# A diffusion block on one Trainium2 core: Hyena spectra from even and odd times, and scan outputs turned within the next group's steps

## The chip, the cores and the metric

The kernel runs on one core of one Trainium2 chip, all in fp32. The metric is the device time of an execution in microseconds. PE is TensorE, DVE is VectorE, ACT is ScalarE, POOL is GpSimd and SP is the engine that issues most of the transfers. The kernel is written instruction by instruction: each engine has its own program, and the programs meet only at semaphores.

## What is computed

One layer of a backbone with 256 latent and 256 context tokens of width 2048. Two parts of it matter here, the Hyena convolution and the output of the gated delta scan:

```python
def hyena_filters(n, w1, b1, w2, b2, w3, b3, freq):
    ...
    filt = filt * jnp.exp(-t[:, None] * deltas[None, :])[:, None, None, :]
    circ = jnp.concatenate([filt[:, 0], jnp.zeros((1, HY_ORDER, HY_W), F32), filt[:0:-1, 1]], axis=0)
    return jnp.fft.rfft(circ, axis=0)

def long_conv(u, filt_f, skip):
    n = u.shape[1]
    y = jnp.fft.irfft(jnp.fft.rfft(u, n=2 * n, axis=1) * filt_f, n=2 * n, axis=1)[:, :n]
    return y + u * skip.astype(F32)

def hyena_mix(p, conv, conv_w, filt_f, skip):
    ...
    y = x1 * long_conv(v, filt_f[:, 0], skip[0])
    return x2 * long_conv(y, filt_f[:, 1], skip[1])

def gated_delta_chunked(q, k, v, g, beta, s0):      # per head and direction, chunks of 64 tokens
    ...
    def step(s, inp):
        q_i, k_i, u_i, w_i, g_i, a_i = inp
        v_new = u_i - jnp.einsum('bhcd,bhdv->bhcv', w_i, s)
        o = jnp.einsum('bhcd,bhdv->bhcv', q_i * jnp.exp(g_i)[..., None], s) + jnp.einsum('bhcm,bhmv->bhcv', a_i, v_new)
        ...
        return s, o

def merge_branches(o_dn, proj, y_hy, norm_w, w_pa, w_ph, w_out):
    z = ...
    o = (rms_norm(o_dn.transpose(0, 2, 1, 3), norm_w) * jax.nn.silu(z)).reshape(b, n, DN_V_W).astype(dt)
    gates = jax.nn.sigmoid(proj[..., OFF_GATE:].astype(F32))
    merged = gates[..., :D_MODEL] * (o @ w_pa) + gates[..., D_MODEL:] * (y_hy.astype(dt) @ w_ph)
    return merged.astype(dt) @ w_out
```

After that come an output projection, a layer norm and the PEER feed-forward, which gathers rows of two expert tables and fills the second third of the time.

## The kernel before

The stages follow each other: modulation, gates, projection and short convolution of 16 heads (to 883 us), gates (to 1092), the 48 Hyena tiles of the combined projection (to 1430), the Hyena convolutions (to 1661), the scan (to 1871), the 32 tiles of the branch projections (to 2096), output projection and norm, and PEER (from 2242). Each Hyena tile of the first 32 is turned to tokens on partitions by two PE transposes (`hy_turn`, L678, from `hacc`).

**Hyena convolutions.** The 2048 channels go in four blocks `n` of 512, and each has two orders `o`, so `convolve(n, o, last)` runs eight times, six of them in a loop. A transform is a product with a constant matrix of cosines or sines: 256 times on the contraction (two halves `t` of 128), 256 frequencies (two halves `f`), 512 channels on the free side. On PE the order in `convolve` is: the filter's spectrum, four banks of two accumulated products each (L710; banks 4, 5 the cosines of the sum filter `fa`, banks 6, 7 the sines of `fb`); the signal's transform, eight products into banks 0 to 3 (L720); `filters` for the next convolution (L700, into banks 4 to 7); the inverse (L733 for o = 0, L740 for o = 1). ACT copies the four banks of the spectrum to `Fr` and `Fi` (L1012, L1013). DVE runs `products` (L1400 to L1408, six operations for each half `f`), then `fold`, which makes the next `fa` and `fb` out of `filters` (L1378 to L1389), then the multiplication by the gate (L1415, or L1420 into `yhT`). PE waits for `fold` before the spectrum (`fil_used`), for the last gate product before the signal (`inv_used`), for the copies before `filters` (`spec_copied`), and for all products before the inverse (`prod_done`).

**Scan.** 16 heads go in four groups of four (`grp`), in a loop of two passes with two groups each (`r`). A group has eight steps `g`: four over the context, four over the latent tokens. In a step PE multiplies keys (and queries) by the states (L771, L774), DVE makes `r_in` (L1446), PE multiplies it by the inverses (L784), ACT copies and scales the result (L1025, L1028), PE multiplies by the attention (L792, latent only) and by the keys (L804), and DVE updates the states (L1466) and adds the outputs to `o_acc` (L1474). The first step of a group has no state and begins with L784. A group ends with: the squares of `o_acc` (L1032) and the root (L1035) on ACT, the reciprocal (L1476) and the scaling (L1481) on DVE, PE's transposes of `o_acc` (L809) and DVE's products with `zsT` (L1488), which count `o_merged`. The first L784 of the next group waits for `o_merged`; so do SP's loads of the inverses of the group after (`inverses_in`, 32 transfers into one of two `invs`), POOL's loads of `att` (one buffer, 16 transfers) and of the records two groups ahead (`rec_load`).

**Branches.** `wide(s, s, ...)` makes one tile of 16 products into bank `s`; its weights come from four slots of `wring`, which share their place with scan records, so SP loads them only after PE has counted `br_proj` at the scan's end. Tiles alternate between delta output (`zsT`) and Hyena output (`yhT`), and DVE multiplies by the gates and adds.

Of the kernel before, what the change touches and what calls it, by code (L numbers as in the profile page):

```python
# [22 lines left out]
ALU = mybir.AluOpType  # L23
# [3 lines left out]
P = 128  # L27
D = 2048
KT = D // P
# [17 lines left out]

CONST_COLS = {}
# [10 lines left out]
def constant_table():  # L59
# [24 lines left out]
    two = lambda a: a.reshape(2, P, SEQ).transpose(1, 0, 2).reshape(P, 2 * SEQ)  # L84
    put("cos", two(np.cos(ang)))
# [9 lines left out]
def build(nc, a, out):  # L95

    with ExitStack() as ctx:
# [136 lines left out]
        yb = area(HT0 + 12288, 2, N1)  # L234
        zT = area(R0 + 17024, SEQ)
# [15 lines left out]
        invs = [area(at, 4, 1024).rearrange("p u (q t w i) -> p u q t w i", q=2, t=2, w=2) for at in (HT0, R0 + 20480)]  # L251
        att = area(R0 + 28672, 4, 512).rearrange("p u (t w i) -> p u t w i", t=2, w=2)
# [8 lines left out]
        tmp_g = area(R0 + 28672, 2, SEQ)  # L261
# [87 lines left out]
        def _(sp):  # L349
# [139 lines left out]
        def _(pe):  # L489
# [213 lines left out]
            def convolve(n, o, last):  # L703
# [19 lines left out]
                if not last:  # L723

                    pe.wait_ge(sem("spec_copied"), c * 4 + 4)
# [26 lines left out]
            with pe.Fori(0, 2) as i:  # L752
                for r in range(2):
# [5 lines left out]
                    for g in range(8):  # L759
# [4 lines left out]
                        for u in range(4):  # L764
# [41 lines left out]
                    for u in range(4):  # L806
                        pe.wait_ge(sem("o_normed"), grp * 8 + (2 * u + 2))
                        for t in range(2):
                            m = nc.tensor.transpose(bank[2 * u + 1][:, (2 + t) * P:(3 + t) * P], o_acc[:, 2 * u + t, :], const("ident"))  # L809
                        m.then_inc(sem("o_turned"), 1)  # L810
# [1059 lines left out]
```

## Time and profile before

| | us |
|---|---|
| three runs | 3635.89, 3638.99, 3639.49 |
| median | 3638.99 |
| profiled execution, its own time | 3637.51 |
| its span | 3636.0 |
| PE busy | 2911.1 (80%) |
| DVE busy | 2172.2 (60%) |
| ACT busy | 393.8 (11%) |
| POOL busy | 977.5 (27%) |
| mean granted clock of PE | 0.882 |

"Idle before" is the time that an engine stood still ahead of an instruction, with the instruction on another engine that ended it; "issue" is waiting that nothing in the trace accounts for.

### The profile page before, as it was taken

To read this page: it belongs to the slowest core of one execution; us is meant where nothing else is said; L and a number is where in the kernel's file an instruction comes from. 1 tells how busy PE (TensorE), PEld (TensorE's weight loads), DVE (VectorE), ACT (ScalarE), POOL (GpSimd) and SP (SyncE) were. 2 spreads that over 40 slices of the span, in tenths; PEclk is the share of its full clock that TensorE was granted. 3 is DMA by queue.
4 is the path that set the end of the run, shared out by engine and by line. 5 is a ranking of instruction groups with operands and counts; after the bars stand their busy time and mean duration, and the time that the engine had idled before them with its cause. 6 is when DMAs were issued, how large, how long until landed. Compare 5 with 4: busy or idle time off the path is not lost.

```text
span 3636.0 us, 33108 instructions
## 1 busy us (share of the span) xinstructions
PE 2911.1 (80%) x10631; PEld 1816.6 (50%) x10631; DVE 2172.2 (60%) x3251; ACT 393.8 (11%) x951; POOL 977.5 (27%) x752
## 2 busy tenths in 40 slices
PE   4899999999999999998789997665565655556555
PEld 1585555556888887445678845542222222222222
DVE  1236767676997122655640013796878778886675
ACT  0121222222000000002310000010000000000000
POOL 0000111111000001001100000377666566666552
PEclk7899999999999999999899998877768677777777
DMA  9335666667444442103324543899999999999997
GB/s 410 150 118 209 225 229 225 241 223 265 172 173 174 150 155 93 35 23 108 103 99 151 207 162 118 342 407 417 422 422 421 421 421 422 385 421 422 421 422 304
DMA packets 146743, 935.09 MB, mean 257 GB/s; under 512 B 35295, under 2 KB 35584, under 8 KB 38356
## 3 DMA queue, kind: packets, MB, share of 16 engines
q0 software_dynamic: 92384, 652.43, 44.2%
q1 hardware_dynamic: 54264, 281.52, 21.1%
q8 instruction: 45, 0.74, 0.1%
q14 instruction: 50, 0.41, 0.0%
HBM read 906.51 MB, written 27.36 MB: 257 GB/s over the span
## 4 chain that ended last, share of the span: by engine, by line
PE 57%; DMA 21%; DVE 10%; issue 6%; POOL 5%; DVEq 0%; ACT 0%; SPq 0%; PEld 0%; POOLq 0%; ACTq 0%; PEldq 0%
PE bank L534 25%; PE bank L595 15%; DMA arena<-peer_v_in,arena 15%; POOL arena L1801 5%; PE bank L865 4%; DMA arena<-peer_u_in,arena 3%; PE bank L831 3%; DMA arena<-w_ada_in 3%; DVE arena L1637 2%; PE bank L710 2%; PE bank L784 1%; DVE arena L1658 1%; PE bank L740 1%; PE bank L733 1%; PE bank L720 1%
## 5 line engine op out<-in xcount | busy, mean ns | idle before, releaser
L865 PE MATMUL bank<-arena 128*128 128x512 f32 x992 | 700.9, 873 | 517.7 <-DMA arena<-peer_v_in,arena 488.2
L534 PE MATMUL bank<-arena 128*128 128x256 f32 x4608 | 1008.4, 381 | 9.2 <-DMA arena<-w_branch_in 5.1
L534 PEld LDWEIGHTS bank<-arena 128*128 128x128 f32 x4608 | 876.2, 191 | 131.2 <-issue 8.7
L865 PEld LDWEIGHTS bank<-arena 128*128 128x128 f32 x992 | 270.4, 286 | 947.5 <-issue 902.7
L1637 DVE CUSTOM_DVE_ANT_0 arena<-arena 128x2048 f32<-128x2048 f32 x256 | 587.0, 2293 | 246.4 <-DMA arena<-peer_u_in,arena 223.5
L1801 POOL DMA_INDIRECT arena<-peer_u_in,arena x256 | 387.0, 1512 | 776.4 <-issue 548.5
L595 PE MATMUL bank<-arena 128*128 128x512 f32 (+1 forms) x1536 | 556.3, 522 | 0.0
L1801 POOL DMA_INDIRECT arena<-peer_v_in,arena x256 | 440.4, 1720 | 163.4 <-issue 74.0
L595 PEld LDWEIGHTS bank<-arena 128*128 128x128 f32 x1536 | 290.7, 190 | 258.8 <-issue 241.8
L1658 DVE SCALAR_TENSOR_TENSOR arena<-arena 128x2048 f32<-128x2048 f32 x130 | 305.7, 2352 | 41.4 <-DMA arena<-peer_v_in,arena 37.3
L1260 DVE CUSTOM_DVE_ANT_0 arena<-arena 128x2048 f32<-128x2048 f32 x64 | 146.6, 2290 | 138.8 <-DMA arena<-w_ada_in 138.8
L1715 POOL DMA_DIRECT2D arena<-w_ada_in x64 | 34.3, 535 | 615.9 <-DVE arena L1260 422.0
L1362 DVE TENSOR_SCALAR arena<-arena 128x256 f32<-128x256 f32 (+1 forms) x48 | 16.9, 352 | 205.2 <-PE bank L678 135.2
L831 PE MATMUL bank<-arena 128*128 128x512 f32 x256 | 112.4, 600 | 9.5 <-DVE arena L1519 8.1
L1334 DVE TENSOR_TENSOR arena<-arena 128x62 f32<-128x62 f32 (+30 forms) x124 | 106.6, 859 | 17.1 <-DMA arena<-beta_scr 12.9
L1337 DVE TENSOR_TENSOR arena<-arena 128x62 f32<-128x62 f32 (+30 forms) x124 | 106.6, 860 | 4.3
L1246 DVE SCALAR_TENSOR_TENSOR arena<-arena 128x256 f32<-128x256 f32 x192 | 91.9, 479 | 9.1 <-DVE arena L1244 2.3
L505 PE MATMUL bank<-arena 128*32 128x512 f32 x256 | 47.4, 878 | 48.2 <-DMA arena<-w_ada_in 48.2
L831 PEld LDWEIGHTS bank<-arena 128*128 128x128 f32 x256 | 48.9, 192 | 72.6 <-issue 61.9
L1068 ACT ACTIVATE arena<-arena 128x16 f32<-128x16 f32 x16 | 3.5, 216 | 704.4 <-DVE arena L1637 704.4
L1272 DVE RECIPROCAL arena<-arena 128x256 f32<-128x256 f32 (+1 forms) x32 | 79.3, 2521 | 0.2 <-DVE arena L1266 0.2
L1766 POOL MEMSET arena<- 128x2048 f32 x1 | 1.8, 1804 | 281.3 <-DVE arena L1364 281.3
(253 smaller groups left out, 2235.8 us busy)
## 6 DMA issues: line engine op xcount, KB each, us to landing
arena<-w_in_in SPq DMA_DIRECT2D x144, 1024.0 KB, 4.8
arena<-w_ada_in POOLq DMA_DIRECT2D x64, 1024.0 KB, 5.1
arena<-w_ada_in SPq DMA_DIRECT2D x16, 2048.0 KB, 17.2
arena<-w_branch_in SPq DMA_DIRECT2D x32, 1024.0 KB, 4.8
rec_scr<-arena POOLq DMA_DIRECT2D x16, 1024.0 KB, 4.6
arena<-rec_scr POOLq DMA_DIRECT2D x16, 1024.0 KB, 7.4
arena<-w_out_in SPq DMA_DIRECT2D x8, 2048.0 KB, 8.2
arena<-w_q_in SPq DMA_DIRECT2D x16, 1024.0 KB, 8.1
```

Of the source, the lines that this page charges most:

```text
L534: m = mm(bank[b][:, 0:SEQ], wring[:, slot, k, :], src[:, k, 0:SEQ], start=(k == 0), stop=(k == KT - 1))
L595: m = mm(bank[t][:, 0:n], wring[:, t, k, :], hT[:, k, 0:n], start=(k == 0), stop=(k == KT - 1))
L831: m = mm(bank[4 + t][:, :], gT[:, s * 8 + k, t * P:(t + 1) * P], wo_ring[:, s, k, :], start=(s == 0 and k == 0), stop=(s == 1 and k == 7))
L865: m = mm(bank[4 * t + j][:, :], diag[:, d % 8, :], ring[buffer[n]][:, j * N1:(j + 1) * N1], start=(d == 0 or d == last_pe[0] + 1), stop=(d ...
L1246: stt(a_lat, x, w(j), a_lat, ALU.mult, ALU.add).then_inc(sem("tap"), 1)
L1260: v.tensor_tensor_reduce(ada_junk, wring[:, 3].rearrange("p k n -> p (k n)"), cond_row, 1.0, 0.0, ALU.mult, ALU.add, ada_dot[:, e:e + 1]). ...
L1272: v.reciprocal(nrm[:, j, 0:n], nrm[:, j, 0:n]).then_inc(sem("recip"), 1)
L1334: tt(tmp, m_[:, j + 1:CH, j:j + 1].broadcast_to([P, rows, j]), m_[:, j:j + 1, 0:j].broadcast_to([P, rows, j]), ALU.mult).then_inc(sem("sol ...
L1337: tt(below, below, tmp, ALU.add).then_inc(sem("solve_step"), 1)
L1637: v.tensor_tensor_reduce(junk, ring[buffer[n]], h2[:, g // PH, :], 1.0, 0.0, ALU.mult, ALU.add, dots[:, g % 2, e:e + 1]).then_inc(sem("row ...
L1658: stt(y, ring[buffer[n]], c_, y, ALU.mult, ALU.add).then_inc(sem("row_dve"), 1)
L1801: pool.indirect_dma_start(ring[buffer[n]], None, a["peer_" + kind], bass.IndirectOffsetOnAxis(ap=idx[:, g // PH, at:at + 1].bitcast(U32), ...
```

## The change

Two things, and some that follow from them.

1. Tokens are put in the order even, then odd, on the contraction, and the upper half of the frequencies is mirrored (`EVEN_ODD`, `MIRRORED`). With that the two halves of a real transform are the sum and the difference of the even tokens' product and the odd tokens' product. The spectrum takes four products in place of eight (each bank holds one, nothing is accumulated), ACT copies the two odd banks only, and DVE makes `Fr` and `Fi` by four additions and subtractions (`spectra`). The signal's transform and the inverse keep their counts; `hy_turn` reads every second token, and the last gate product (L1420) reads its bank with a step of 128.
2. The end of group `grp` is moved into group `grp + 1`: squares on ACT after the copies of steps 0 and 1, the root after step 1, reciprocal and scaling on DVE at the end of step 1, transposes on PE in step 3 after each head's state products, and the products with `zsT` on DVE in step 3 before each head's `r_in`. The first L784 of a group waits for the additions of the one before only. The loop over groups is written out, so heads are constants. SP's and POOL's loads wait for `av_ready`, the last attention product of the group.
3. The branch tiles of each four are now two of Hyena, then two of delta output, so that the first two can run while the last group's outputs are finished; its transposes stand between tiles 0 and 1. DVE's operations on them are in the new order, without `tmp_g`.

```diff
+EVEN_ODD = np.arange(SEQ).reshape(P, 2).T.reshape(-1)
+MIRRORED = np.concatenate([np.arange(P), np.arange(SEQ - 1, P - 1, -1)])
...
+    ang = ang[EVEN_ODD][:, MIRRORED]
...
+        def out_at(grp, u, t):
+
+            return bank[4 + u][:, t * P:(t + 1) * P] if grp == 3 else bank[2 * u + t][:, (3 - t) * P:(4 - t) * P]
...
-                sp.wait_ge(sem("o_merged"), 5 + 4 * (grp - 1))
+                sp.wait_ge(sem("av_ready"), 16 * (grp - 1))
...
-                    m = nc.tensor.transpose(bank[4 + s][:, t * P:(t + 1) * P], hacc[:, s, t * P:(t + 1) * P], const("ident"))
+                    m = nc.tensor.transpose(bank[4 + s][:, t * P:(t + 1) * P], hacc[:, s, t::2], const("ident"))
...
-                for f in range(2):
-                    for src, w, b in ((fa, "cos", 4), (fb, "sin", 6)):
-                        for t in range(2):
-                            m = mm(bank[b + f][:, :], const(w)[:, t * SEQ + f * P:t * SEQ + (f + 1) * P], src[:, t, :],
-                                   start=(t == 0), stop=(t == 1))
+                for src, w, b in ((fa, "cos", 4), (fb, "sin", 6)):
+                    for t in range(2):
+                        m = mm(bank[b + t][:, :], const(w)[:, t * SEQ:t * SEQ + P], src[:, t, :], start=True, stop=True)
                     m.then_inc(sem("spec_ready"), 1)
...
+            def turn_out(grp, u):
+                pe.wait_ge(sem("o_normed"), grp * 8 + (2 * u + 2))
+                for t in range(2):
+                    m = nc.tensor.transpose(out_at(grp, u, t), o_acc[:, 2 * u + t, :], const("ident"))
+                m.then_inc(sem("o_turned"), 1)
...
+                            if g == 3 and grp:
+                                turn_out(grp - 1, u)
...
-                                pe.wait_ge(sem("o_merged"), 5 + grp * 4)
+                                if grp:
+                                    pe.wait_ge(sem("o_added"), grp * 32)
...
             pe.sem_inc(sem("br_proj"), 4)
+
+            def branches(i, s):
+                weights_in(s, i + 24)
+                pe.wait_ge(sem("br_used"), 1 + i * 4 + s)
+                wide(s, s, yhT if s < 2 else zsT).then_inc(sem("br_proj"), 1)
+
+            pe.wait_ge(sem("o_added"), 4 * 32)
+            branches(0, 0)
+            for u in range(4):
+                turn_out(3, u)
+            branches(0, 1)
             pe.wait_ge(sem("o_merged"), 5 + 16)
...
+                    for i in range(2):
+                        act.wait_ge(sem("spec_ready"), n * 4 + (2 * o + i + 1))
+                        act.wait_ge(sem("spec_copied"), n * 8 + (1 + 4 * o))
+                        af(odds[:, i, :], bank[5 + 2 * i][:, :], ACT.Copy).then_inc(sem("odd_copied"), 1)
...
+                    if grp and g < 2:
+                        squares(grp - 1, 2 * g)
+                        squares(grp - 1, 2 * g + 1)
+                        if g == 1:
+                            deviations(grp - 1)
...
+            def spectra(n, o):
+
+                c = n * 2 + o
+                for i, (F, b) in enumerate(((Fr, 4), (Fi, 6))):
+                    dve.wait_ge(sem("odd_copied"), c * 2 + (i + 1))
+                    even = bank[b][:, :]
+                    tt(F[:, 0, :], even, odds[:, i, :], ALU.add).then_inc(sem("spec_copied"), 1)
+                    if i == 0:
+                        tt(F[:, 1, :], even, odds[:, i, :], ALU.subtract).then_inc(sem("spec_copied"), 1)
+                    else:
+                        tt(F[:, 1, :], odds[:, i, :], even, ALU.subtract).then_inc(sem("spec_copied"), 1)
...
-                        tt(x, bank[b][:, 0:SEQ].unsqueeze(1), x, ALU.mult).then_inc(sem("inv_used"), 1)
+                        x = x.rearrange("p o (n t) -> p (o n) t", t=2)
+                        tt(x, bank[b][:, 0:SEQ].rearrange("p (t n) -> p n t", t=2), x, ALU.mult).then_inc(sem("inv_used"), 1)
...
+                            if g == 3 and grp:
+                                merge_out(grp - 1, u)
                             dve.wait_ge(sem("ks_ready"), grp * 28 + ((g - 1) * 4 + u + 1))
...
+                        if g == 1 and grp:
+                            normalize_out(grp - 1)
+            normalize_out(3)
+            for u in range(4):
+                merge_out(3, u)
```

`squares`, `deviations`, `normalize_out` and `merge_out` hold the operations that stood at a group's end, unchanged.

## Rows read from the trace of the kernel before

**Rows 1.** The page's chain that ended last: shares of the span by line.
```profile
PE bank L534 25%; PE bank L595 15%; DMA arena<-peer_v_in,arena 15%; POOL arena L1801 5%; PE bank L865 4%; DMA arena<-peer_u_in,arena 3%; PE bank L831 3%; DMA arena<-w_ada_in 3%; DVE arena L1637 2%; PE bank L710 2%; PE bank L784 1%; DVE arena L1658 1%; PE bank L740 1%; PE bank L733 1%; PE bank L720 1%
```
**Rows 2.** Windows: stretch, length; PE, PEld, DVE, ACT, POOL busy; granted clock, DMA, GB/s.
```profile
1440.37:1660.24 219.87, 205.13 (x504) 103.69 (x504) 113.35 (x182) 17.36 (x32) 9.42 (x17) 0.93 0.14 40
1661.11:1703.61 42.50, 38.63 (x384) 29.02 (x384) 29.34 (x116) 13.53 (x48) 5.46 (x5) 1.00 0.38 125
1712.07:1754.79 42.72, 39.92 (x384) 30.69 (x384) 29.59 (x116) 12.57 (x47) 11.61 (x20) 0.95 0.45 137
1763.96:1808.11 44.15, 40.89 (x384) 31.37 (x384) 29.80 (x116) 13.53 (x48) 9.88 (x18) 0.92 0.44 131
1816.58:1859.83 43.25, 40.50 (x384) 31.31 (x384) 29.77 (x116) 12.58 (x47) 9.47 (x16) 0.94 0.05 14
1859.83:1870.87 11.04, 1.97 (x9) 1.38 (x9) 3.93 (x17) 2.91 (x15) 0.00 (x0) 0.64 0.39 143
1542.00:1548.00 6.00, 5.37 (x13) 4.29 (x14) 5.71 (x10) 0.00 (x0) 0.00 (x0) 0.50 0.00 0
```
**Rows 3.** Chain in order of time, 1496 to 1556 us: start, length, what.
```profile
1498.25 6.87 PE bank L710 x16
1505.12 3.45 PE bank L720 x8
...
1516.87 7.13 PE bank L733 x16
1524.01 6.87 PE bank L710 x16
...
1542.63 10.22 PE bank L740 x32
```
**Rows 4.** Timeline, 1496 to 1556 us: start, length, instructions, idle before them in brackets.
```profile
1501.81 0.60 ACT L1012 ACTIVATE arena<-bank 128x512 f32<-128x512 f32 x1 [24.42 <-PE bank L710]
...
1508.78 0.69 DVE L1400 TENSOR_TENSOR arena<-bank,arena 128x512 f32<-128x512 f32 x1 [9.94 <-PE bank L720]
...
1516.87 7.13 PE L733 MATMUL bank<-arena 128*128 128x512 f32 x16 [1.46 <-DVE arena L1408]
```
**Rows 5.** Timeline, the end of the first group.
```profile
1702.97 0.31 ACT L1032 ACTIVATE arena<-arena 128x128 f32<-128x128 f32 x1 [0.36 <-DVE arena L1474]
...
1706.43 1.28 ACT L1035 ACT_TABLE_LOAD   x1
...
1708.29 1.66 DVE L1481 TENSOR_SCALAR arena<-arena 128x128 f32<-128x128 f32 x8
...
1709.87 2.15 DVE L1488 SCALAR_TENSOR_TENSOR arena<-bank,arena 128x128 f32 x8
```
**Rows 6.** Timeline, steps 1 and 2 of the second group.
```profile
1717.74 1.14 ACT L1025 ACTIVATE arena<-bank,arena 128x128 f32<-128x128 f32 x4 [3.09 <-PE bank L784]
...
1718.94 2.22 DVE L1466 SCALAR_TENSOR_TENSOR arena<-arena,bank 128x128 f32<-128x128 f32 x8 [1.12 <-PE bank L804]
...
1723.33 2.15 DVE L1466 SCALAR_TENSOR_TENSOR arena<-arena,bank 128x128 f32<-128x128 f32 x8 [1.12 <-PE bank L804]
```
**Rows 7.** Chain in order of time, from the second group to the third.
```profile
1761.94 2.02 issue
...
1766.07 0.05 ACTq L1025
```
**Rows 8.** Turned and straight operands on DVE (lines' own view), then the projection's chain.
```profile
L1344 DVE TENSOR_TENSOR arena<-arena x2: 7233/7240/7246, 1016.2 to 1139.0; 64x4096 f32<-64x4096 f32 x2
L1345 DVE TENSOR_TENSOR arena<-arena x2: 4422/4422/4422, 1023.5 to 1146.3; 64x4096 f32<-64x4096 f32 x2
1161.36 6.91 PE bank L534 x32
1168.49 6.91 PE bank L534 x32
```
**Rows 9.** Timeline, the end of the scan: SP's loads of branch weights.
```profile
1865.41 22.81 SPq L452 DMA_DIRECT2D arena<-w_branch_in  x6
```

More of the change, by code:

```diff
@@ L805, in _ @@
                                 m.then_inc(sem("upd_ready"), 1)
[L806 to L810, printed above, removed]
-            pe.sem_inc(sem("br_proj"), 4)
+            pe.sem_inc(sem("br_proj"), 4)
+            def branches(i, s):
[7 more added lines that the diff above has]
+            branches(0, 1)
             pe.wait_ge(sem("o_merged"), 5 + 16)
-            with pe.Fori(0, 8) as i:
+            branches(0, 2)
+            branches(0, 3)
+            with pe.Fori(1, 8) as i:
                 for s in range(4):
-                    weights_in(s, i + 24)
-                    pe.wait_ge(sem("br_used"), 1 + i * 4 + s)
-                    wide(s, s, (zsT, yhT)[s % 2]).then_inc(sem("br_proj"), 1)
+                    branches(i, s)
             pe.sem_inc(sem("wo_used"), 2)
@@ new lines, in _, with squares @@
+                    for i in range(2):
+                        act.wait_ge(sem("spec_ready"), n * 4 + (2 * o + i + 1))
+                        act.wait_ge(sem("spec_copied"), n * 8 + (1 + 4 * o))
+                        af(odds[:, i, :], bank[5 + 2 * i][:, :], ACT.Copy).then_inc(sem("odd_copied"), 1)
+            def squares(grp, u):
+                act.wait_ge(sem("o_added"), grp * 32 + (24 + 4 + u + 1))
+                for t in range(2):
+                    af(o_sq, o_acc[:, 2 * u + t, :], ACT.Square, accum_out=o_ss[:, 2 * u + t:2 * u + t + 1]
+                       ).then_inc(sem("o_ss"), 1)
+                    act.wait_ge(sem("o_ss"), grp * 9 + (2 * u + t + 1))
@@ L1036, in _ @@
+            for u in range(4):
+                squares(3, u)
+            deviations(3)
             for t in range(2):
@@ L1428, in _, with normalize_out, merge_out @@
             dve.wait_ge(sem("hpads"), 2)
-            with dve.Fori(0, 2) as i:
+            def normalize_out(grp):
+                dve.wait_ge(sem("o_ss"), grp * 9 + 9)
+                v.reciprocal(o_ss, o_ss).then_inc(sem("o_rstd"), 1)
+                dve.wait_ge(sem("o_rstd"), grp + 1)
+                for u in range(4):
+                    for t in range(2):
+                        oa = o_acc[:, 2 * u + t, :]
+                        ts(oa, oa, o_ss[:, 2 * u + t:2 * u + t + 1], None, ALU.mult).then_inc(sem("o_normed"), 1)
+            def merge_out(grp, u):
+                dve.wait_ge(sem("o_turned"), 1 + grp * 4 + (u + 1))
+                z_ = zsT[:, 4 * grp + u, :].rearrange("p (c n) -> p c n", c=NCH)
+                for t, zz in ((0, z_[:, 0::3, :]), (1, z_[:, 1:3, :])):
+                    m = stt(zz, out_at(grp, u, t).rearrange("p (c n) -> p c n", c=2), dn_nw[:, 0:1], zz,
+                            ALU.mult, ALU.mult)
+                m.then_inc(sem("o_merged"), 1)
+            for i in range(2):
                 for r in range(2):
@@ L1474, in _ @@
                                 tt(oa, bank[2 * u + 1][:, P:2 * P], oa, ALU.add).then_inc(sem("o_added"), 1)
-                    dve.wait_ge(sem("o_ss"), grp * 9 + 9)
-                    v.reciprocal(o_ss, o_ss).then_inc(sem("o_rstd"), 1)
-                    dve.wait_ge(sem("o_rstd"), grp + 1)
-                    for u in range(4):
-                        for t in range(2):
-                            oa = o_acc[:, 2 * u + t, :]
-                            ts(oa, oa, o_ss[:, 2 * u + t:2 * u + t + 1], None, ALU.mult).then_inc(sem("o_normed"), 1)
```

90 lines of the change are left out of this document (35 added, 55 removed).

## The prediction

> **What bounds the kernel now.** I read the page's chain of work that ended last first [rows 1]: PE's matmul lines lead it and DMA of the expert tables follows, so the time is a row of stages, each with its own limit, and a stage that gets shorter moves all later ones. Two stages are touched, and the windows give them [rows 2]: the Hyena convolutions, 219.87 us for eight of them, and the scan, four groups of heads with bodies of 42.50, 42.72, 44.15 and 43.25 us, gaps between them of 8.46 (1703.61 to 1712.07), 9.17 and 8.47, and 11.04 from the last body to the first branch matmul. In the windows of the bodies PE is busy over 90% of the time, but that counts pipelined latencies; so inside a stage I go by the chain of waits in order of time.
>
> In a convolution the chain is [rows 3]: spectra of the filter on PE (L710, 6.87 us for eight 128x512 products, two records each), the first half of the signal's transform (L720, 3.45), some 8.3 us of products on DVE while PE finishes the other half and the next filter (1508.56 to 1516.87), and the inverse on PE (L733, 7.13, or L740, 10.22). One convolution is 25.76 us (1498.25 to 1524.01); its partner is longer by what L740 is longer than L733. DVE sat idle 9.94 us before its products and the copies of ACT take 0.60 each [rows 4]: all of the spectra is on PE's side of the chain.
>
> In the scan each of a body's first four steps is a ring PE, DVE, PE, ACT, PE, DVE, 4.39 us long (the updates of the states begin at 1718.94 and 1723.33), with no engine the bound [rows 6]; the last four are longer rings of the same kind. Between groups the ring is empty: ACT squares o_acc, takes a root, DVE scales (L1481), PE turns, DVE merges (L1488), and only then does PE begin the next group [rows 5].
>
> **Spectra.** Removed: 4 of 8 products on PE per convolution. 6.87 / 8 = 0.86 each, so 3.43 us, at the head of the chain, with nothing else at work beside them. Added: ACT copies two odd banks in place of four, DVE makes four sums. Where do they lie? Let a convolution start at 0. The cosine pair is ready at 1.7, the sine pair at 3.4; ACT adds 0.6 to each; a 512-wide DVE operation comes every 0.6 to 0.7 (the run of products above has 12 in 8.3). The sums end near 5.5. The first half of the signal's transform now ends at 3.43 + 3.45 = 6.9. So 1.4 us of slack hides the sums in DVE's former idle time, of which 9.94 becomes about 6.5 less 2.7. If that cover were gone the four sums would cost up to 2.7 us each convolution, and the gain would fall to under 1. DVE's load for a convolution goes from 14.2 us (113.35 / 8 [rows 2]) to some 17 of 22.3, so it doesn't become the bound; PE waits for the products as before. Late next is what was late before: the products. The other order of frequencies, the even-odd windows and the once longer wait of PE's filters on the sums (queued behind it: only the inverse, which waits for the products anyhow) change no length. 8 x 3.43 = 27.4 us.
>
> **Strides.** The reads of odd or even tokens are the unknown costs. DVE: L1420's operand is now read with its inner step 128 elements long. The nearest rows are the same multiply of 64x4096 with turned operands, 7.24 us, and with straight ones, 4.42 [rows 8]: 2.82 / 4096 = 0.69 ns an element, so 0.18 us for 256, between 0 and 0.18; three of four hide under the next of PE's products, and the fourth is on the path only at the end: 0.2 us at most, which I take. PE: 64 transposes of the projection (L678) now read every second element. That stage is PE's alone: a tile comes every 7.13 us, of which 6.91 are its product and 0.22 a pair of transposes [rows 8]. No row has a PE operand with such a step; bounds are 0 and doubling, 32 x 0.22 = 7.0 us; a gain has no way to arise, since as many elements pass. I take 0, since the plain transposes are the nearest row, and keep 7.0 for the range. The Trainium skill speaks for 0 ("SBUF — State Buffer", Door 1, the note on cachelines): an SBUF line has 16 bytes and two hits in it are enough for the full rate, which a step of two fp32 gives. By it the sum stays; no row here shows it.
>
> **Scan, removed.** The three gaps go: 8.46 + 9.17 + 8.47 = 26.1, of which 0.1 each stays, since PE's first product of a group now waits only for the sums of the one before. The 9.17 has the loop's way back in it, which the unrolled code lacks; so I set all of it at nothing. Group one has no slow start but waits about 1.2 for a table load in ACT (1.28 [rows 5]): a clean body is 41.3. The others ran at a granted clock of 0.95, 0.92 and 0.94, because PE had stood still in the gap [rows 2], and lost 1.4 to 2.9 each. Unrolled, the registers that picked the head go too: in the step they stood on the chain before ACT's first operation, 0.05 us [rows 7], and in the same way before DVE's, with an issue of that size beside each. That is an estimate of 0.2 a step (bounds 0.1 and 0.3), for 7 steps of 4 groups: 5.6 us.
>
> **Scan, added.** The step is a ring, so whatever DVE does between two of its turns is paid whole. After step 1: reciprocal 0.2 and L1481, 1.66 [rows 5]: 1.9 us, ahead of L1446 of step 2, for which PE waits (its inverse products queue behind). Is the root ready? ACT has 3.09 idle before a step [rows 6]; eight squares took from 1702.97 to 1706.43, so four take 1.7, and fit beside step 0; four and the root, 2.0, fit beside step 1. But a table load in front of the root makes it 3.3 and DVE waits 1.15. Before, ACT loaded two tables in each pass of the loop over two groups (at its first copy, and at the root [rows 5]); straight code needs the second once: only the second group pays. In step 3: PE's two transposes for each head (0.22, as in the projection) fit between its products with the states, which come with the states, every 2.15 / 4 = 0.54 [rows 6]; DVE's two merges for each head come before that head's L1446: 2.15 us in all [rows 5], paid whole. So bodies: 42.5; 41.3 + 1.9 + 2.15 + 1.15 = 46.5; 45.35; 45.35. With 0.3 for three joints 180.0, against 198.72: 18.7 less, and the 5.6 of registers.
>
> PE now stands still twice in a group, 2 to 3 us, where before it stood 8 once. At the end of each product phase it idled 1.46 us [rows 4], and after every second one it was granted 0.50, the 1.2 GHz level [rows 2], so that L740 took 10.22 where L733, with as many columns, took 7.13 [rows 3]. So such stops can cost the clock. I allow two falls at the 2 us that the slow bodies lost: 4 us. Scan: 18.7 + 5.6 - 4.0 = 20.3 less.
>
> ScalarE's tables have a rule of their own. "ScalarE activation tables: per-element evaluation and per-set limits" in the Trainium skill ("Table sets in the compiler and the runtime") says that loads are placed per block, by the longest run. By it one set with the root would be loaded at the group's first copy and the 1.15 would go; the trace speaks against it, with two loads in one pass.
>
> **DMA and queues.** The inverses' loads (SP, 32 issues of some 0.75 us) and att and rec (GpSimd, 9.5 and 2.2 us) wait for the last att product instead of the merge, so they start some 8 us earlier, with the group that needs them: the lead is the same. Behind them on SP are only the branch weights. Nothing there waited before.
>
> **Tail.** The branch weights' slots hold records of the scan, so they can only be loaded when PE is done; the load was issued at 1865.41, after the transposes, and PE began 5.46 later, at 1870.87 [rows 2, 9]. Now it goes out at the end of the body: first branch product 5.2 later, and 1.1 for the last group's transposes within the branch products, whose merges hide behind 13.7 us of two Hyena tiles. 11.04 - 5.2 - 1.1 - 0.3 (slow clock for the turns) = 4.4 less. The order of the 32 branch tiles changes no count.
>
> **Sum.** 27.4 - 0.2 + 20.3 + 4.4 = 51.9. The profiled execution took 3637.51 (span 3636.0 and 1.5 around it), 1.5 under the median of 3638.99: 3637.5 - 51.9 = 3585.6, and I say 3586.
>
> **Rivals.** A, the clock: each stop of PE in the scan (six) and one stop in every convolution rather than in every second costs a fall: 4 more at 2 and 4 at 3.1 us, 20 back: 3606. For it: 0.50 after only 1.46 us of idle. Against: that came after every second phase alone (L733 kept its 7.13 [rows 3]). Halfway, some of them, 3596. B, the sums in the convolution come late (ACT's copy, a bank that is read while PE writes its neighbour), 2.7 x 8 = 21.6 back: 3607. Against: 1.4 us of slack. C, the falls of the convolutions vanish, since PE's phases shift: 4 x 3.1, and none in the scan, 4: 3570. D, slower: straight code must be fetched, and the one jump between groups cost 2.02 us of issue in the second gap [rows 7]. If fetching stopped an engine so at every part of the code, 26 stops would use up the 52 us; nine in each group, 36, cost 73: 3659. Against: a pass of the loop is straight code already, 384 records of PE in each body [rows 2], and its steps repeat alike. E, the change doesn't do what it says: the gap's work costs in the steps what it cost in the gap, so that the scan gains only the registers: 3637.5 - 27.2 - 4.4 - 5.6 = 3600.
>
> **How the numbers follow.** Forecast with its own spread (3578 to 3594) 0.52; A in full or in part 0.18; B 0.06; C 0.10; E 0.08; D 0.03; something that I don't see and that uses up the gain to within 0.2% 0.03. The range takes the forecast, the halfway part of A, E and most of C, with 7.0 for PE's strides: 3571 to 3603. A difference of 0.2% (7 us) is about what a measurement can tell from none; the chances are 0.94 faster, 0.03 same, 0.03 slower.
>
> **What would show it.** L710 with 64 records and 3.4 us a convolution, periods near 22.3 and 25.4; DVE's sums before its products and no wait for ACT there; no gap over 0.5 us between groups; steps 1 and 3 longer by 1.9 and 2.1; one root load; branch products 5.2 after the last sum. Wrong if the wait before the products goes to the sums, if the granted clock is 0.50 inside a group, or if a projected tile takes more than 7.13.

## The result, and the profile after

| | before | after |
|---|---|---|
| median, us | 3639.24 (3635.89 to 3641.24) | 3587.95 (3582.61 to 3588.68) |
| ratio | 1 | 0.9854, 95% interval 0.9841 to 0.9866 |
| profiled execution, span | 3637.51, 3636.0 | 3588.51, 3586.9 |
| PE, DVE, ACT busy | 2911.1, 2172.2, 393.8 | 2873.1, 2191.5, 382.8 |
| mean granted clock of PE | 0.882 | 0.889 |

The change makes the kernel 51.3 us faster, 1.5%. 3586 was predicted.

The windows of the kernel after follow, with the columns of [rows 2]: the convolutions up to the scan's first product, the four bodies, the tail, the branches.

```profile
1441.84:1637.23 195.39, 180.19 (x440) 90.95 (x440) 134.06 (x215) 9.56 (x16) 9.46 (x17) 0.92 0.15 45
1637.23:1677.55 40.32, 37.80 (x384) 28.25 (x384) 29.34 (x116) 11.67 (x44) 5.65 (x6) 1.00 0.40 132
1677.70:1723.92 46.22, 40.84 (x392) 30.27 (x392) 33.35 (x133) 16.50 (x62) 11.49 (x21) 0.96 0.43 127
1724.07:1769.13 45.06, 40.95 (x392) 30.61 (x392) 33.17 (x133) 15.51 (x61) 11.55 (x21) 0.96 0.42 129
1769.28:1815.36 46.08, 41.96 (x392) 31.16 (x392) 33.35 (x133) 16.00 (x64) 9.37 (x16) 0.93 0.04 13
1815.36:1819.76 4.40, 0.00 (x1) 0.04 (x1) 1.20 (x7) 2.91 (x15) 0.00 (x0) 0.96 0.90 322
1819.76:2044.87 225.11, 223.62 (x1033) 196.34 (x1033) 23.12 (x60) 0.00 (x0) 0.00 (x0) 0.99 0.50 176
```

Against the kernel before, stage by stage, from the same edges in both traces (its convolutions up to the scan's first product are 1440.37 to 1661.11, its scan 1661.11 to 1859.83, and the first product of its output projection comes at 2096.30, in the kernel after at 2044.87):

| | before | after | change | predicted |
|---|---|---|---|---|
| ahead of the first spectrum | 1440.37 | 1441.84 | +1.47 | 0 |
| convolutions | 220.74 | 195.39 | -25.35 | -27.2 |
| scan, first product to last sum | 198.72 | 178.13 | -20.59 | -20.3 |
| tail and branch tiles | 236.47 | 229.51 | -6.96 | -4.4 |
| after them | 1539.70 | 1542.03 | +2.33 | 0 |
| sum | 3636.0 | 3586.9 | -49.1 | -51.9 |

**Convolutions.** The chain of the kernel after in order of time (start, length, what):

```profile
1508.07 8.83 PE bank L741 x16
1516.90 3.43 PE bank L719 x8
...
1532.10 8.86 PE bank L748 x32
```

The spectrum has half of its records and takes 3.43 us where it took 6.87 [rows 3]. Both inverses (L741, L748) take 8.8 us. Before, they took 7.13 and 10.22 in turn [rows 3]. The timeline of the same convolution (start, length, engine, instructions, idle before them) has the sums:

```profile
1518.74 0.60 ACT L1033 ACTIVATE arena<-bank 128x512 f32<-128x512 f32 x1 [21.78 <-PE bank L719]
1519.37 0.69 DVE L1428 TENSOR_TENSOR arena<-bank,arena 128x512 f32<-128x512 f32 x1 [1.61 <-ACT arena L1033]
1521.61 0.68 DVE L1432 TENSOR_TENSOR arena<-arena,bank 128x512 f32<-128x512 f32 x1
1524.00 0.69 DVE L1443 TENSOR_TENSOR arena<-bank,arena 128x512 f32<-128x512 f32 x1 [1.71 <-PE bank L728]
```

The last sum ends at 1522.29, and the first product (L1443) then waits 1.71 us for PE's L728. So the sums lie in time that DVE had free, with 1.7 us to spare. Two neighbouring convolutions start 24.02 and 24.05 us apart (1492.88, 1516.90, 1540.95), where they were 25.76 and 28.85.

**Scan.** The timeline of the kernel after, steps 0 to 3 of the second group:

```profile
1677.70 1.13 PE L801 MATMUL bank<-arena 128*128 128x128 f32 x8 [0.48 <-DVE arena L1537]
...
1684.80 1.28 ACT L1043 ACT_TABLE_LOAD   x1
...
1686.43 0.20 DVE L1475 RECIPROCAL arena<-arena 128x8 f32<-128x8 f32 x1 [1.18 <-ACT arena L1043]
1686.67 1.66 DVE L1480 TENSOR_SCALAR arena<-arena 128x128 f32<-128x128 f32 x8
...
1688.64 1.36 PE L801 MATMUL bank<-arena 128*128 128x128 f32 x8 [2.90 <-DVE arena L1509]
...
1689.93 2.08 PE L821 MATMUL bank<-arena 64*128 64x128 f32 x16
...
1694.06 0.60 DVE L1486 SCALAR_TENSOR_TENSOR arena<-bank,arena 128x128 f32<-128x128 f32 x2
```

The next group's first product (L801) now comes 0.15 us after the sum, at 1677.70. The price is in the ring: DVE waits 1.18 us for the root and its table, then scales (L1480), and PE stands still for 2.90 us. After that stop sixteen key products (L821) take 2.08 us. In step 0 they take 1.16. In groups three and four no load stands there, and the stop is 1.63 us. After this stop the granted clock is down in each of the three groups: 0.50 from 1690 to 1692, 0.51 from 1734 to 1736, 0.50 from 1780 to 1784. In step 3 PE stops for 0.29 us at most. The row of L1486 is one of four pairs of merges that stand in step 3.

**Tail.** Timeline of the kernel after, the scan's end:

```profile
1814.73 14.18 SPq L462 DMA_DIRECT2D arena<-w_branch_in  x5
...
1819.76 8.64 PE L544 MATMUL bank<-arena 128*128 128x256 f32 x32 [4.73 <-issue]
1828.23 1.04 PE L763 MATMUL bank<-arena 128*128 128x128 f32 x8
1828.65 2.16 DVE L1486 SCALAR_TENSOR_TENSOR arena<-bank,arena 128x128 f32<-128x128 f32 x8 [8.23 <-PE bank L763]
```

The branch weights are asked for with the last attention product, at 1814.73, 0.63 us before the last sum's end, and PE begins 5.03 us after 1814.73. [rows 9] had the load at 1865.41, 5.58 us after the last sum. The turns (L763) are on PE's path, and the merges are beside tile 1.

### The profile page after: what moved, and what is told of

It reads as the page before. It is cut to its first block, busy times and chain, and to the rows that moved or that the text cites. A ratio compares the mean times of both kernels' runs of the same rounds, so it can differ in the third digit from the quotient of the medians.

```text
span 3586.9 us, 31709 instructions
## 1 busy us (share of the span) xinstructions
PE 2873.1 (80%) x10567; PEld 1797.9 (50%) x10567; DVE 2191.5 (61%) x3283; ACT 382.8 (11%) x932; POOL 990.2 (28%) x752
## 4 chain that ended last, share of the span: by engine, by line
PE 56%; DMA 20%; DVE 14%; issue 5%; POOL 4%; ACT 0%; DVEq 0%; SPq 0%; POOLq 0%; ACTq 0%
PE bank L544 25%; PE bank L605 15%; DMA arena<-peer_v_in,arena 12%; DMA arena<-peer_u_in,arena 5%; POOL arena L1852 4%; DVE arena L1688 4%; PE bank L852 3%; PE bank L886 3%; DMA arena<-w_ada_in 3%; DVE arena L1709 2%; PE bank L801 1%; DVE arena L1529 1%; PE bank L748 1%; PE bank L741 1%; PE bank L719 1%
## 5 line engine op out<-in xcount | busy, mean ns | idle before, releaser
L886 PE MATMUL bank<-arena 128*128 128x512 f32 x992 | 691.4, 862 | 528.1 <-DMA arena<-peer_v_in,arena 508.4
L1852 POOL DMA_INDIRECT arena<-peer_u_in,arena x256 | 399.2, 1559 | 766.3 <-issue 548.0
L852 PE MATMUL bank<-arena 128*128 128x512 f32 x256 | 112.6, 601 | 9.6 <-DVE arena L1570 8.1
```

The source lines that it names most:

```text
L852: m = mm(bank[4 + t][:, :], gT[:, s * 8 + k, t * P:(t + 1) * P], wo_ring[:, s, k, :], start=(s == 0 and k == 0), stop=(s == 1 and k == 7))
L886: m = mm(bank[4 * t + j][:, :], diag[:, d % 8, :], ring[buffer[n]][:, j * N1:(j + 1) * N1], start=(d == 0 or d == last_pe[0] + 1), stop=(d ...
L1852: pool.indirect_dma_start(ring[buffer[n]], None, a["peer_" + kind], bass.IndirectOffsetOnAxis(ap=idx[:, g // PH, at:at + 1].bitcast(U32), ...
```

## The experiments

Each ran against the kernel before on the same chip: e1, e2 and e6 on one chip (the kernel before took 3640.67 there), the others on a second one (3639.84, and 3643.59 beside e5, which ran later). The table gives the times; the edits and what follows stand below it.

| kernel | median, us (lowest to highest) | ratio to before, 95% interval |
|---|---|---|
| e1_spectra_only | 3614.32 (3609.89 to 3618.36) | 0.9925, 0.9909 to 0.9942 |
| e2_scan_only | 3613.71 (3612.51 to 3614.92) | 0.9927, 0.9911 to 0.9944 |
| e6_unrolled | 3629.15 (3626.46 to 3631.53) | 0.9968, 0.9955 to 0.9981 |
| e0_after_again | 3585.33 (3583.80 to 3587.55) | 0.9849, 0.9833 to 0.9866 |
| e3_rows128 | 3578.11 (3576.26 to 3579.96) | 0.9829, 0.9812 to 0.9845 |
| e4_hidden | 3574.41 (3571.85 to 3577.80) | 0.9819, 0.9802 to 0.9835 |
| e7_filler | 3579.67 (3578.49 to 3584.09) | 0.9832, 0.9816 to 0.9849 |
| e5_hidden_rows128 | 3566.80 (3562.18 to 3566.96) | 0.9793, 0.9777 to 0.9808 |

**The two parts alone.** e1 is the kernel before with part 1 of the change (four products, copies of the odd banks, sums, even and odd order). e2 is the kernel after with part 1 undone:

```diff
-                for src, w, b in ((fa, "cos", 4), (fb, "sin", 6)):
-                    for t in range(2):
-                        m = mm(bank[b + t][:, :], const(w)[:, t * SEQ:t * SEQ + P], src[:, t, :], start=True, stop=True)
+                for f in range(2):
+                    for src, w, b in ((fa, "cos", 4), (fb, "sin", 6)):
+                        for t in range(2):
+                            m = mm(bank[b + f][:, :], const(w)[:, t * SEQ + f * P:t * SEQ + (f + 1) * P], src[:, t, :],
+                                   start=(t == 0), stop=(t == 1))
```

> The kernel before with the spectra part alone. Theory 1 (each part shortens its own stretch of the chain, and the stretches add up): 3.43 us of products go from the head of each convolution, and the brief clock falls that the changed kernel shows after every convolution (8.83 in place of 7.13 us for the inverse, eight times, in place of 10.22 three times) give some 2 back, so the stretch from the first spectrum to the scan is 25 us shorter and the median near 3614 us. The scan starts each group after a gap of 8.5 us as before. Theory 2 (the sums of DVE come late and eat the gain, and the measured gain is the scan's): under 8 us, 3632 or more. Shown by the idle time of DVE before its first product: 1.7 us by theory 1, none by theory 2.

> The changed kernel with eight spectra products again, token order as before; scan, tail and branch order changed. Theory 1: scan 178 us from its first product to the last sum in place of 199, first branch product 4.4 us later in place of 11, a fall of the clock less in the branch products: 27 us shorter, 3612 us. Together with the other half 52, against the 51 measured for both. Theory 2 (parts don't add, since the clock falls by phase): the two halves' sum misses the whole by over 6 us.

Measured beside one median of before, 3640.67: 26.4 us less and 27.0 us less. Their sum, 53.3, is that of the whole change (51.3 in one comparison, 54.5 in the other). So the parts add. The first was priced at 27.2, the second at 20.3 + 4.4 = 24.7, some 2 too little. Windows of e1, then of e2, convolutions and scan:

```profile
1440.70:1636.45 195.75, 180.15 (x440) 90.89 (x441) 134.06 (x215) 9.57 (x16) 9.61 (x18) 0.92 0.16 45
1636.45:1838.43 201.98, 167.47 (x1560) 127.76 (x1560) 130.24 (x515) 64.07 (x234) 38.25 (x61) 0.91 0.28 88
```
```profile
1438.40:1660.87 222.47, 207.26 (x504) 103.05 (x504) 113.47 (x183) 17.36 (x32) 9.37 (x16) 0.93 0.13 39
1660.87:1837.26 176.39, 159.20 (x1560) 118.69 (x1560) 129.14 (x515) 59.56 (x231) 38.30 (x61) 0.98 0.32 100
```

The gain of part 1 stands in the convolutions and that of part 2 in the scan and tail. e1's profiled run, 3616.69, has a scan 3.3 us longer than before, though its scan is the one before. 2.0 of that lie between the starts of the third and the fourth group (54.64 us against 52.62); the wait of PE for nothing that the trace shows, in the loop's way back, is nearly the same (3.49 us against 3.25). The cause stays open, and with it how far the scan's length differs between executions of one program. e2 has the scan of the kernel after and took 176.39 us for it, 1.7 less than that kernel's 178.13: the granted clock fell in two of its groups, not in three.

**The loop written out, nothing moved.** e6 is the kernel before with the scan's loop over groups as plain code and heads as constants, in the programs of PE, ACT and DVE:

```diff
-            with act.Fori(0, 2) as i:
+            for i in range(2):
...
-                                af(v_tail[:, u, :], B, ACT.Copy, scale=mixed[:, 4 + s // 2, T, bass.ds(h, 1)]
+                                af(v_tail[:, u, :], B, ACT.Copy, scale=mixed[:, 4 + s // 2, T, h:h + 1]
```

> The kernel before with only the loop over the scan's groups written out and heads as constants; every group still ends in its gap. Theory 1 (the registers stand on the ring's path, 0.2 us a step): bodies of 41.1 us or less in place of 42.5 to 44.2, 5.6 us for the registers, 2.0 for the way back of the loop, 1 to 2 for a table load: 9 us shorter, 3630. Rival (registers are worked out beside waiting): only the way back and the load, 3 us, 3636.

Measured: 11.5 us less. Windows of e6, the convolutions and the four bodies:

```profile
1436.80:1659.35 222.55, 207.34 (x504) 103.12 (x504) 113.47 (x183) 17.39 (x32) 9.45 (x17) 0.93 0.13 40
1659.35:1699.67 40.32, 37.80 (x384) 28.25 (x384) 29.34 (x116) 12.29 (x47) 5.62 (x5) 1.00 0.39 132
1708.25:1749.74 41.49, 39.00 (x384) 29.64 (x384) 29.34 (x116) 12.62 (x47) 11.65 (x20) 0.96 0.46 140
1757.03:1799.32 42.29, 39.80 (x384) 30.62 (x384) 29.71 (x116) 12.61 (x47) 11.65 (x20) 0.93 0.45 138
1806.62:1848.10 41.48, 38.99 (x384) 29.89 (x384) 29.33 (x116) 12.61 (x47) 9.49 (x16) 0.95 0.05 14
```

Its scan is 188.75 us, 9.97 under the 198.72 of before, so half of the scan's gain comes from writing the loop out and not from the move of the outputs. The clean body is 40.32 us, to the hundredth that of the kernel after, at the same granted clock of 1.00. 42.50 was a body with a table load in it, for which PE waited 1.18 us ahead of its key products at 1663.45; e6 has no load there (ACT has 47 instructions instead of 48). So of the 2.18 between them 1.2 is the load. The other 1.0 is put down to the registers; no run takes the registers out and leaves the loop.

Its convolutions are those of the kernel before in code, but not in their pattern of the clock. The chain of e6:

```profile
1458.16 8.83 PE bank L733 x16
...
1485.62 8.86 PE bank L740 x32
```

**Are the convolutions' slow stretches bound to their stops?** PE's last work before its 1.46 us stop are the next filters, eight records whose operands have 65 rows (L710 of the kernel after). e3 gives these products all 128 rows, the added ones zeros, so that as many products take as long (median 592 ns in both kernels), over all rows of PE:

```diff
-                        m = mm(bank[4 + 2 * d + t][:, :], hid2[0:65, t * P:(t + 1) * P], w3c[0:65, 2 * d + o, :], start=True, stop=True)
+                        m = mm(bank[4 + 2 * d + t][:, :], hid2[:, t * P:(t + 1) * P], w3c[:, 2 * d + o, :], start=True, stop=True)
...
+                    v.memset(hid2[CH:P, :], 0.0).then_inc(sem("hid_zero"), 1)
+                    dve.wait_ge(sem("hid_zero"), 1)
```

> The changed kernel with the filters' products (L710) over 128 rows in place of 65, the added rows of one operand zero; as many products, as long, same result. What makes the granted clock fall to 0.50 after each product phase? Theory A (the 3.6 us of 65-row products before the stop belong to its cause): the clock stays at 1.00, the inverses take 7.1 in place of 8.8, 8 x 1.7 = 14 us less for the seven that follow filters: 3576 us. Theory B (the stop of 1.46 us alone): no change, 3588.

Measured: 7.2 us less than the kernel after. Chain and window of the convolutions in e3:

```profile
1460.49 7.13 PE bank L741 x16
...
1482.82 7.17 PE bank L748 x32
...
1616.51 9.89 PE bank L748 x32
```
```profile
1442.20:1626.90 184.70, 169.45 (x440) 85.88 (x441) 133.82 (x215) 9.55 (x16) 9.43 (x17) 0.97 0.16 48
```

The stop is still there, 1.46 us ahead of L748, but the seven inverses that follow filters take 7.13 and 7.17 where they took 8.83 and 8.86. The last one (1616.51) has no filters ahead of it and a stop of 4.70 us in both kernels; it takes 9.89 where it took 8.88. The convolutions are 10.7 us shorter. So a slow stretch does not follow from the stop of 1.46 us alone; what PE ran right before it decides too. Not all of the 10.7 reaches the median: the profiled execution of e3 is 7.0 us shorter than that of e0_after_again, with 0.8 more in the scan and 1.6 and 1.5 more ahead of the convolutions and behind the branch tiles, where the two kernels hardly differ.

**What do the stops in the scan cost?** e7 is the kernel after with work for PE in step 2 of the last three groups, ahead of the last head's products with the states, into a part of a bank that nobody reads. It adds products whose results go nowhere:

```diff
+                            if grp and g == 2 and u == 3:
+                                for k in range(8):
+                                    mm(bank[7][:, 2 * P:3 * P], const("ident"), const("ones"), start=True, stop=True)
```

> The changed kernel with eight more products on PE (identity by ones, results unused) before the last head's state products in step 2 of groups two to four, where PE now stands for 1.9 to 2.9 us. Theory 1 (the stop alone costs the clock, and the slow clock then costs the step): granted clock 1.00 through the group, bodies 1 to 1.7 us shorter each, 3584 us. Rival (the clock's fall is free since the ring waits for DVE anyhow): clock 1.00 but no change of time, 3588; or the fillers delay the ring, 3590.

Measured: 5.7 us less than e0_after_again. Timeline of e7 in step 2 of the second and of the third group, then its last three bodies:

```profile
1688.99 1.26 PE L804 MATMUL bank<-arena 128*128 128x128 f32 x8 [0.92 <-DVE arena L1512]
...
1731.19 2.05 PE L786 MATMUL bank<-arena 128*128 128x128 f32 x16
```
```profile
1678.05:1723.44 45.39, 41.65 (x408) 31.20 (x408) 33.27 (x133) 16.53 (x62) 11.46 (x21) 1.00 0.42 129
1723.59:1767.88 44.29, 41.48 (x408) 31.09 (x408) 33.26 (x133) 15.25 (x61) 11.52 (x21) 1.00 0.44 132
1768.03:1812.34 44.31, 41.48 (x408) 31.09 (x408) 33.30 (x133) 15.85 (x64) 9.37 (x16) 1.00 0.05 13
```

The added products (L786) run for 2.05 us, beside DVE's scaling. So they lie in the stop itself: of its 2.90 us 0.92 are left in the second group, and in the third PE goes on without one. The granted clock is 1.00 in all three bodies. Against the kernel after they are 0.83, 0.77 and 1.77 shorter, 3.4 us together: that is what three falls of the clock cost there. The profiled execution was the slowest of e7's four and is only 1.6 us under that of e0_after_again: its scan is 3.4 us shorter, but its branch tiles are 1.7 us longer (226.65 against 225.00), with a granted clock of 0.78 in their first 14.13 us against 0.90. Where the rest of the 5.7 comes from can't be seen.

**Can the outputs' work be hidden?** e4 puts it where DVE waits: the root's reciprocal and half of the scalings in step 2, the rest in step 3, between `r_in` and the update of the states; two heads are turned and merged in step 3 and two in step 4.

```diff
-                            if g == 3 and grp:
+                            if grp and g == 3 + u // 2:
                                 merge_out(grp - 1, u)
...
+                        if grp and g in (2, 3):
+                            if g == 2:
+                                root_out(grp - 1)
+                            scale_out(grp - 1, 2 * (g - 2))
+                            scale_out(grp - 1, 2 * (g - 2) + 1)
...
-                        if g == 1 and grp:
-                            normalize_out(grp - 1)
```

> The changed kernel with the reciprocal and the scaling of the last group's outputs on DVE moved out of the path: not after step 1 but into DVE's waits for PE of steps 2 and 3 (1.02 us each), half in each; two heads are turned and merged in step 3, two in step 4. Theory 1 (the ring pays DVE's work whole where it stands between two of its turns, nothing where it stands in a wait): 3 x 1.9 us and the 1.2 of the wait for the root go, and with the stop its clock fall, some 1.5 each: 11 us less, 3577. Rival (the waits are not free: PE's products of the same step slow, or the clock falls elsewhere): under 5 us, 3583 or more.

Measured: 10.9 us less than e0_after_again. The last three bodies of e4, and DVE's timeline in its step 2:

```profile
1676.87:1719.28 42.41, 39.08 (x392) 29.16 (x392) 33.17 (x133) 16.35 (x62) 11.49 (x21) 1.00 0.45 138
1719.44:1761.71 42.27, 39.03 (x392) 29.11 (x392) 33.17 (x133) 15.18 (x61) 11.50 (x21) 1.00 0.46 138
1761.86:1804.11 42.25, 39.01 (x392) 29.09 (x392) 33.16 (x133) 15.78 (x64) 9.30 (x16) 1.00 0.05 14
```
```profile
1685.60 0.20 DVE L1475 RECIPROCAL arena<-arena 128x8 f32<-128x8 f32 x1
1685.84 0.96 DVE L1481 TENSOR_SCALAR arena<-arena 128x128 f32<-128x128 f32 x4
1686.63 2.15 DVE L1540 SCALAR_TENSOR_TENSOR arena<-arena,bank 128x128 f32<-128x128 f32 x8
```

The scalings stand without idle time between `r_in` and the states. The clock falls went with the stop. Against e7, where the clock was 1.00 too, the bodies are 2.98, 2.02 and 2.06 shorter: the scaling (with the load's wait in the first) is hidden. Against the clean body of 40.32 they are still 2.0 longer, which is about the length of the merges.

**Both.** e5 has the edits of e3 and e4.

> The changed kernel with both of the last edits: the filters' products over all 128 rows (the rows from 65 on hold zeros), and the normalisation and merges of a group's heads within waits of VectorE and spread over the next group's steps 2 to 4. If the two gains are apart, each in its own stage, the convolutions keep the 10.7 us that the first gave them there (195.4 to 184.7) and the scan the 10.4 that the second gave it (178.1 to 167.7): 3585.3 - 10.7 - 10.4 = 3564 us, or 3567 if only the medians' differences (7.2 and 10.9) add. If they don't add, because the slow stretch of TensorE only moves from one stage to the other, it stays near the better one alone, 3574 us.

Measured: 3566.8 us. That is 18.5 less than e0_after_again, where e3 and e4 alone gave 7.2 and 10.9, so they add. (e5 was timed later than these; by the ratios to the kernel before, 0.9793 and 0.9849, it is 20 us.) Windows of e5, convolutions and scan:

```profile
1441.90:1626.72 184.82, 169.61 (x440) 85.92 (x440) 133.80 (x215) 9.56 (x16) 9.46 (x17) 0.97 0.16 47
1626.72:1794.44 167.72, 154.94 (x1560) 115.73 (x1560) 128.85 (x515) 58.98 (x231) 38.41 (x61) 1.00 0.34 105
```

It beats both kernels: 0.9793 of the time before, against 0.9849 for the change in a run on the same chip.

**The change again.**

> The changed kernel once more, beside the next three on the same chip: 3588 us, with the inverses at 8.8 us, one clock fall in each of the last three groups.

Measured: 3585.33 us. The predicted 3586 lies between the two medians of the change.

## Why the prediction was right

Its sum was 51.9; the profiled executions differ by 49.1, the medians by 51.3 and 54.5. The mechanism held in both stages: the spectra's products left the chain and their sums didn't enter it, and the gaps between the groups closed at the priced cost in the steps. That the median is met to 0.6 us is in part luck. Between the two profiled executions the convolutions gained 1.9 less than forecast and the tail 2.6 more, the stretches that the change leaves alone lost 3.8, and inside the scan errors of 1.7, 1.2 and 0.6 cancelled. Term by term:

**Spectra, 27.4: right.** Against the 220.74 of the profiled execution before, the convolutions gained 25.35. Against e2 and e6, which run the eight products with one slow stretch after every stop as the kernel after does, they gained 222.5 - 195.4 = 27.1. The missing 1.8 is in the main the clock's pattern. Before, three of L740 took 10.22 [rows 3] and the last less, by the chain of the kernel before:

```profile
1651.47 8.75 PE bank L740 x32
```

That is 3 x 3.09 + 1.62 = 10.9 over 7.13. In the kernel after eight inverses cost 1.7 each, 13.7. That is 2.8 more. The chain gives the rest: the first spectrum took 10.13 before (9.62 in e6) and 6.41 after, all at a lowered clock, so it gained 3.72; the other seven gained 3.44 each; and from the last inverse's end to the scan's first product it is 0.89 before and 0.50 after (and in e6). 3.72 + 24.1 + 0.4 - 2.8 = 25.4. The stretch of products on DVE is 8.1 to 8.3 us in both. The slack for the sums was put at 1.4 and is 1.71.

**Strides, 0.2 and 0: right in the sum, wrong in the operation.** The gate product takes 0.42 us with either step (median 424 ns in both kernels), so it costs nothing. The transposes do cost, but hardly on the chain. Lines' own views of L678 of before and L688 of after, the weight loads (columns: count, shortest/median/longest ns, first and last start), then one tile late in each chain:

```profile
L678 PEld LDWEIGHTS bank<-arena x64: 139/141/143, 1153.6 to 1374.8; 128*128 128x128 f32 x64
...
1375.19 55.27 PE bank L534 x256
```
```profile
L688 PEld LDWEIGHTS bank<-arena x64: 196/196/201, 1154.8 to 1376.3; 128*128 128x128 f32 x64
...
1205.37 6.91 PE bank L544 x32
...
1376.65 55.27 PE bank L544 x256
```

A load with a step of two takes 196 ns instead of 141, beside other products. It goes with the order of tokens: e1 has 196 too, and e2 has 141. The 24 tiles from 1205.37 to 1376.65 take 7.137 each; before, the 30 from 1161.36 [rows 8] to 1375.19 took 7.128. So it is 0.3 us in 32 tiles. "SBUF — State Buffer" of the Trainium skill (Door 1) would have no loss at this step; the load's row is against that, though the kernel's time hardly shows it.

**Scan, 178.4 us: right to 0.3, by terms that offset each other.** Its sum was 180.0 less 5.6 for the registers plus 4.0 for the clock. The gaps, the table load ahead of the root, the scaling and the merges came out as priced: e7's three bodies exceed 3 x 40.32 by 13.03, against 5.7 + 6.45 + 1.15 = 13.3, and the joints took 0.45 for 0.3. Mis-sized were three terms. The registers were put at 5.6 and gave 3.9 (the four bodies without loss and without the load, 42.5 + 3 x 41.3 - 1.2, less 4 x 40.32), 0.14 a step, if all that is left there belongs to them. The load at the first copy was kept in the sum and is gone, 1.2 (the kernel after has one load in the whole scan, the one at 1684.80). And the clock fell three times, not twice, at 3.4 us together where 4 stood; in e2's execution of the same scan it fell twice. The forecast had PE stand still for 2 to 3 us twice in each group; it did so once, 2.90 and 1.63 us in step 2, while the merges in step 3 left stops of 0.29.

**The tables' rule.** The prediction went by the trace against "ScalarE activation tables: per-element evaluation and per-set limits" in the Trainium skill ("Table sets in the compiler and the runtime"), by which the longest run decides and the wait before the root would go. The trace after agrees with the choice: the load stands at the root, and DVE waited 1.18 us there, for 1.15 priced. But the reason given was two loads in one pass of the loop. Written out, the scan has a single load, and the prediction missed that the one at the first copy goes.

**Tail, 4.4: too small by 2.6.** The gap is 4.40 where 5.2 was priced, 0.8 less, of which 0.63 is that the load waits for the last product, not for the sum. The branch tiles, with 1.04 of turns among them, take 225.11 where they took 225.43 without, so that 1.4 of cost became 0.3 of gain: 1.7. Most of that is no merit of the change. e1 and e6 run the tail of the kernel before, and their tiles take 224.3 us in both, 1.2 less than in the profiled execution of the kernel before. The clock goes with it: in the first 14.13 us of the tiles 0.80 was granted in the kernel before, 0.88 in e1 and e6, and 0.89 in the kernel after. Measured against e1 and e6 the turns and the new order cost 0.8 us where 1.4 was priced, and the whole tail gained 5.0 to 5.4 us, 1 us more than 4.4. Why the same tail had a longer slow stretch in one execution stays open.

**Ahead and behind, 0: +1.5 and +2.3.** Neither belongs to the change as far as the runs show. The first spectrum begins at 1436.8 to 1442.3 over the ten profiled executions, before, after and the eight above, and from the last branch tile to the end they take 1539.0 to 1543.3. Kernels with the old order of tokens begin earlier (1436.8, 1438.4, 1440.4) than those with the new one (1440.6 to 1442.3). 0.3 of this is the strided loads; the rest is open.

**The rivals.** A saw its condition come true in the convolutions, with a slow stretch after each of eight stops, and by half in the scan, with three of the six. It was wrong in its price: it took 3.1 for each added one, but the stretch after every stop costs the inverse 1.7 us, and that after every second 3.1, so that eight cost 13.7 and four had cost 10.9. B: the first product waits for PE's transform, not for the sums. C: the stretches did not vanish by themselves; e3 and e5 made all but the last vanish, which was worth 10.7 us in that stage. D: no body of e6 is longer than its counterpart in the loop, and e6, whose scan is straight code, is 11.5 us faster. E: the scan gained 20.6, of which e6 has 10.0 and the move of the outputs the other 10.6.

**The signs it named.** DVE's sums came before its products, the joints are 0.15 us, and there is one load at the root. The two periods of the convolutions are 24.02 and 24.05, not 22.3 and 25.4, since every inverse is slowed alike. Two of the three signs of being wrong did show: the granted clock was 0.50 inside three groups, and a projected tile took 7.137 us. Neither moved the sum by much, since 4 us stood in it for the one and the other came to 0.3.

## What to carry to other kernels

Where a step is a ring of engines, look for the place in it where each engine waits: the same 1.9 us of scaling cost 2.0 us at the end of a step and nothing that shows between two operations of the next steps (e4 against e7). Write a short loop out before judging what a rearrangement in it gained; here that alone was half of the scan's gain. And price a clock fall by the stretch that follows, not by the number of stops. Two edits test it: give PE work over more rows just ahead of the stop (e3), or put work into the stop itself (e7).

## What the runs showed of the hardware that was not expected

- The same code showed two patterns of TensorE's clock. With a stop of 1.46 us after most product phases, the profiled execution of the kernel before spent 10.22 us on every second inverse (8.75 on the last) and 7.13 on the others, and e6, whose convolutions are the same instructions, 8.8 us on each. The stage took 220.7 us in the one and 222.5 in the other.
- Products over 128 rows in place of 65 ahead of that stop kept the granted clock up over it: 7.13 and 7.17 us for seven of the eight inverses, 10.7 us for the stage, at no cost in the products' own time (592 ns each in both).
- Eight added products in stops of 1.63 to 2.90 us kept the clock at 1.00 through the scan and brought 3.4 us there. The branch tiles behind them took 1.7 us longer in that execution.
- A table load at the top of a loop's body (ACT, 1.28 us, of which PE waited 1.18) was gone in straight code, and so was 1.0 us more in a body of 42 us, which is put down to register work.
- A 128x128 weight load of every second element took 196 ns where one of neighbouring elements in the same place took 141.
